# Hybrid decoder step, tail of the MoE: residual and expert rows of five token tiles summed by TensorE in PSUM

## The reference

```
h = x + concat(conv_out, rwkv_out) @ w_out
h = h + hier_moe(rmsnorm(h, norm2_g), ...)        # top-2 experts of a token
y = h * rsqrt(mean(h * h) + 1e-6) * norm_f_g      # final RMSNorm, per token
```

## Time and profile before

| | |
|---|---|
| time, median of 3 runs | 1180.86 us (1178.79 to 1181.15) |
| profiled execution: time | 1179.14 us |
| profiled execution: span of the core | 1177.4 us |
| busy: PE, DVE, ACT, POOL | 95%, 57%, 31%, 19% of the span |
| chain that ended last: PE, DVE, DMA | 81%, 9%, 4% of the span |
| granted TensorE clock, mean | 0.978 |
| y_rows reads (line 739) | 8 of 1024 KB and 1 of 512 KB |
| output writes (line 735) | 8 of 512 KB and 1 of 256 KB |

### The profile page before, as it was taken

How to read it: one execution, slowest core, us unless ns; L and a number is a source line. 1 busy time by engine, 2 the same in 40 slices (tenths; PEclk the granted TensorE clock), 3 DMA queues, 4 the chain that set the end, 5 groups by cost and what they waited for, 6 DMA issues and landing times.

```text
span 1177.4 us, 24390 instructions
## 1 busy us (share of the span) xinstructions
PE 1114.6 (95%) x9472; PEld 678.4 (58%) x9473; DVE 676.6 (57%) x1147; ACT 367.5 (31%) x722; POOL 223.6 (19%) x280
## 2 busy tenths in 40 slices
PE   6999999999998789999999999977999999999986
PEld 4666666666666789889894455544333333333362
DVE  6288999983554677888743232465343434334327
ACT  6000011011313657777551221022223232323233
POOL 7000000010002123322320001002233333323100
PEclk9999999999999899999999999977999999999999
DMA  9211111010000111111232421157998899999657
GB/s 290 72 36 36 36 36 45 18 42 23 1 1 6 18 20 20 18 17 18 48 111 98 130 72 36 45 208 295 388 349 322 310 333 340 415 417 400 258 187 311
DMA packets 97293, 171.44 MB, mean 146 GB/s; under 512 B 44377, under 2 KB 68624, under 8 KB 87921
## 3 DMA queue, kind: packets, MB, share of 16 engines
q1 hardware_dynamic: 89713, 152.31, 36.4%
q0 software_dynamic: 7488, 17.84, 4.3%
HBM read 153.63 MB, written 25.91 MB: 152 GB/s over the span
## 4 chain that ended last, share of the span: by engine, by line
PE 81%; DVE 9%; DMA 4%; issue 2%; ACT 2%; SPq 1%; DVEq 0%; ACTq 0%; POOLq 0%
PE ps L1630 27%; PE ps L2090 14%; PE ps L1940 9%; PE ps L2120 7%; PE ps L1642 6%; PE ps L1663 2%; PE ps L2077 2%; DMA arena<-in_w_exp_up_dram 2%; DVE arena L2419 1%; PE ps L2138 1%; PE ps L1970 1%; PE ps L1651 1%; DMA arena<-in_w_exp_down_dram 1%; DVE arena L2422 1%; PE ps L2147 1%
## 5 line engine op out<-in xcount | busy, mean ns | idle before, releaser
L1630 PE MATMUL ps<-arena 128*128 128x384 f32 (+1 forms) x1040 | 319.1, 468 | 0.0
L1630 PEld LDWEIGHTS ps<-arena 128*128 128x128 f32 x1040 | 196.9, 190 | 119.0 <-issue 1.9
L2090 PE MATMUL ps<-arena 128*64 x416 | 188.5, 596 | 3.1 <-DVE arena L2836 1.2
L2093 PE MATMUL ps<-arena 128*64 128x512 f32 x416 | 188.5, 596 | 0.0
L2233 DVE SCALAR_TENSOR_TENSOR arena<-arena,cw 128x1024 f32<-128x1024 f32 x240 | 168.2, 777 | 0.4
L2090 PEld LDWEIGHTS ps<-arena 128*64 128x64 f32 x416 | 54.4, 136 | 111.8 <-issue 111.7
L1940 PE MATMUL ps<-arena 128*128 128x512 f32 x256 | 113.1, 596 | 0.0
L1642 PE MATMUL ps<-arena 64*64 64x64 f32 x2960 | 100.8, 221 | 6.5 <-DMA arena<-x_blocks 2.1
L1642 PEld LDWEIGHTS ps<-arena 64*64 64x64 f32 x2960 | 94.0, 136 | 10.1 <-issue 5.1
L2120 PE MATMUL ps<-arena 128*64 x208 | 96.5, 607 | 2.4 <-ACT arena L1401 2.4
L2123 PE MATMUL ps<-arena 128*64 128x512 f32 x208 | 96.5, 607 | 0.0
(11 more groups left out here) (360 smaller groups left out, 1554.6 us busy)
## 6 DMA issues: line engine op xcount, KB each, us to landing
arena<-in_w_exp_gate_dram SPq DMA_DIRECT2D x32, 1024.0 KB, 8.2
arena<-in_w_exp_up_dram SPq DMA_DIRECT2D x32, 1024.0 KB, 11.3
arena<-in_w_exp_down_dram SPq DMA_DIRECT2D x32, 1024.0 KB, 10.2
arena<-in_w_in_dram SPq DMA_DIRECT2D x22, 512.0 KB, 4.1
arena<-in_x_prompt_dram SPq DMA_DIRECT2D x16, 512.0 KB, 7.9
arena<-y_rows SPq DMA_DIRECT2D x8, 1024.0 KB, 15.0
arena<-in_w_out_dram SPq DMA_DIRECT2D x2, 2048.0 KB, 10.7
xn_rows<-arena SPq DMA_DIRECT2D x8, 512.0 KB, 2.8
```

The source lines that it names most:

```text
L1630: ins = pe.matmul(banks(proj_bank(q) + piece)[:, 0:n1 - n0], win[q % 6][:, c, :], xnT[:, c, n0:n1], start=(c == 0), stop=(c == DC - 1))
L2090: pe.matmul(banks(b)[0:HS, :], xgT[b][:, c, 0:HS], wring_gu[:, bass.ds(slot, 1), 0:2, c, :].rearrange("p a w f -> p (a w) f"), start=(c == ...
L2093: ins = pe.matmul(banks(b)[HS:P, :], xgT[b][:, c, HS:P], wgu[b][:, :, c, :], start=(c == 0), stop=(c == DC - 1))
```

## The change

The residual of five tiles goes into PSUM as well, by an identity matmul, so that VectorE's addition for them is gone; ScalarE's square and VectorE's last multiplication then read these tiles from PSUM (`summed(i)`). TensorE's list has five tiles instead of six: tile 7 moves to VectorE. The identity multiplications ahead are 24 instead of 72, and the residual matmuls of the first four tiles follow them, before the waits for the diagonals and `yk`. The fifth tile (6) reuses the banks of tile 1, for which TensorE waits on `fin_done` 3. The order of processing becomes [0, 8, 1, 2, 3, 4, 5, 7, 6]; the reads keep their order, in a list READ of their own. On VectorE combine(0) and combine(8) come first, combine(4) after last_scale(2), and combine(7) after last_scale(5).

```diff
-        LAST = [0, NT - 1, 1, 2, 3, 4, *range(5, NT - 1)]
-        ON_PE = [1, 2, 3, 5, 6, 7]
+        READ = [0, NT - 1, *range(1, NT - 1)]
+        LAST = [0, NT - 1, 1, 2, 3, 4, 5, 7, 6]
+        ON_PE = [1, 2, 3, 5, 6]
+        ON_DVE = [i for i in LAST if i not in ON_PE]
...
+        def summed(i):
+            return banks(rows_bank(i), 2) if i in ON_PE else hres[i][0:rows_of(i), :]
...
@@ SP
-            for i in LAST:
+            for i in READ:
                 r = rows_of(i)
                 sp.dma_start(yk[i][0:r, :, :], y_pairs[i * P:i * P + r, :, :]).then_inc(yk_in[i], 16)
...
@@ ScalarE
-                act.wait_ge(ff_done, n + 1)
-                act.activation(fin_sq[i][0:r, :], hres[i][0:r, :], ACT.Square, accum_out=stat[0:r, 0, i:i + 1])\
+                if i in ON_PE:
+                    act.wait_ge(rows_psum, NT + ON_PE.index(i) + 1)
+                else:
+                    act.wait_ge(ff_done, ON_DVE.index(i) + 1)
+                act.activation(fin_sq[i][0:r, :], summed(i), ACT.Square, accum_out=stat[0:r, 0, i:i + 1])\
...
@@ TensorE
-            for n in range(72):
+            def residual_in(i):
+                for half in range(2):
+                    pe.matmul(banks(rows_bank(i) + half), ident[:, :], hres[i][:, half * 512:half * 512 + 512],
+                              start=True, stop=False)
+
+            for n in range(24):
                 pe.matmul(banks(7)[:, 0:P], ident[:, :], ident[:, :], start=True, stop=True)
+            for i in ON_PE[0:4]:
+                residual_in(i)
             for n, i in enumerate(ON_PE):
                 b = rows_bank(i)
                 pe.wait_ge(diag_ready, 2 + n)
+                if n == 4:
+                    pe.wait_ge(fin_done, LAST.index(ON_PE[0]) + 1)
+                    residual_in(i)
                 pe.wait_ge(yk_in[i], yk_0[i] + 16)
-                if n >= 4:
-                    pe.wait_ge(ff_done, LAST.index(ON_PE[n - 4]) + 1)
                 for half in range(2):
                     for k in range(TOPK):
                         ins = pe.matmul(banks(b + half), diag[:, k, i, :], yk[i][:, k, half * 512:half * 512 + 512],
-                                        start=(k == 0), stop=(k == TOPK - 1))
+                                        start=False, stop=(k == TOPK - 1))
                 ins.then_inc(rows_psum, 1)
...
@@ VectorE, combine(i)
-                if i in ON_PE:
-                    dve.wait_ge(rows_psum, NT + ON_PE.index(i) + 1)
-                    dve.tensor_tensor(hres[i], banks(rows_bank(i), 2), hres[i], ALU.add).then_inc(ff_done, 1)
-                    return
...
@@ VectorE, last_scale(n)
-                dve.wait_ge(ff_done, n + 1)
-                dve.scalar_tensor_tensor(out=fin[i][0:r, :], in0=hres[i][0:r, :], scalar=stat[0:r, 3, i:i + 1],
+                dve.scalar_tensor_tensor(out=fin[i][0:r, :], in0=summed(i), scalar=stat[0:r, 3, i:i + 1],
                                          in1=gain_f[0:r, :], op0=ALU.mult, op1=ALU.mult).then_inc(fin_done, 1)
 
-            for n in range(NT + 2):
-                if n < NT:
-                    combine(LAST[n])
-                if n >= 2:
-                    last_scale(n - 2)
+            combine(LAST[0])
+            combine(LAST[1])
+            for n in range(NT):
+                last_scale(n)
+                if n == 2:
+                    combine(4)
+                if n == 5:
+                    combine(7)
```

More of the change, by code:

```diff
@@ L493, in hybrid_decoder_step @@
         diag = at(O_ZS + NT * D, TOPK, NT, P)
-        LAST = [0, NT - 1, 1, 2, 3, 4, *range(5, NT - 1)]
-        ON_PE = [1, 2, 3, 5, 6, 7]
+        READ = [0, NT - 1, *range(1, NT - 1)]
+        LAST = [0, NT - 1, 1, 2, 3, 4, 5, 7, 6]
+        ON_PE = [1, 2, 3, 5, 6]
+        ON_DVE = [i for i in LAST if i not in ON_PE]
+        assert len(ON_PE) == 5 and len(LAST) == NT
         diag_ready, rows_psum = tanh_done, gb_psum
```

## The result

| | before | after |
|---|---|---|
| time, median (4 runs each) | 1180.11 us (1178.79 to 1181.15) | 1170.04 us (1167.56 to 1171.63) |
| ratio, 95% interval | | 0.9926 [0.9906, 0.9945] |
| profiled execution: time, span | 1179.14, 1177.4 us | 1171.15, 1169.4 us |

The kernel became faster in this comparison: the ratio is 0.9926, and the medians lie 10.1 us apart. Two later comparisons with the same changed program gave 0.9958 [0.9939, 0.9978] (after_again) and 0.9943 [0.9927, 0.9959] (after_again2). So the effect is nearer to 0.4 to 0.7%.

The account below looks back on a forecast made before the run. TensorE's late start and VectorE's load set the end, with reads beneath. Last read 1160.9 plus 10.6 us of writes gives 1171.5, span 1171.9 against 1177.4: 5.5 us less, 1175.4 from median 1180.86; range 1173.3 to 1178.0.

Parts of the forecast that it names:

- the residuals lie under the wait for tile 1: TensorE after the identities: four tiles' residuals, 6.9 us, cost nothing because tile 1's read lands only at 1144.9.
- A spell at half clock behind the pause: TensorE after its 1.8 us pause: one spell at 1.2 GHz takes 1.7 us of progress, hidden by the writes.
- PSUM operands cost the same: ScalarE's squares and VectorE's scalings reading PSUM: -0.04 to 0 and -0.06 to 0 us each, taken as 0.
- VectorE's load: VectorE in the tail: six additions gone, 6.8 us; tile 7 summed by itself added, 2.55 us.
- The writes last 10.6 us from the last read, and come last: Output writes queued behind the reads: from 1160.9 they take 10.6 us, the last landing at 1171.5, after the engines' 1171.1.
- The reads are unchanged, the last at 1160.9: Reads of the tail's tiles: same landings as before the change, 2.4 us apart, the last at 1160.9.
- The spread of 1180.86 (-2.1, +0.3): Whole kernel: the median before the change and its own spread, used for the forecast time and the range.
- reads did not give way to writes: Rival, DMA in the tail: earlier writes push tile 7's read to 1164.0, gain only 3.6 us, 1177.3; chance 0.12.
- PSUM reads did not slow each other: Rival, engines sharing PSUM: each of five scalings takes 1.2 us more, gain 2.2 to 2.5 us, 1178.4; chance 0.08.
- the clock did not stay at half: Rival, TensorE after its pauses: stays at 1.2 GHz, each tile 6.9 us, 11.2 us slower, 1192.1; chance 0.06.

Follow-up runs that it names:

- after72: The changed kernel with 72 identity matmuls again instead of 24; median 1179.40 us, ratio to the kernel before 1.0009, tail 48.99 us.
- after_dup: The changed kernel with one more 512 KB write, issued behind the first output write; median 1173.32 us, ratio to the kernel before 0.9962, tail 42.09 us.
- after_resdve: The changed kernel with VectorE adding the residual again, in the old VectorE call order; median 1177.76 us, ratio to the kernel before 0.9997, tail 47.81 us.
- after_act8: The changed kernel with tile 8's read issued by ScalarE on its own queue; median 1170.47 us, ratio to the kernel before 0.9938, tail 42.46 us.
- after0: The changed kernel without the 24 identity matmuls; median 1174.15 us, ratio to the kernel before 0.9951, tail 42.46 us.
- before24: The kernel before with 24 instead of 72 identity matmuls, nothing else changed; median 1178.60 us, ratio to before 0.9998, tail 47.90 us.
- before_wide: The kernel before with 19 identity matmuls of 512 columns replacing 72 of 128; median 1178.50 us, ratio to before 1.0005, tail 47.61 us.
- after_read8: The changed kernel with tile 8's read third instead of second; median 1173.04 us, ratio to the kernel before 0.9948, tail 41.07 us.

## Why the prediction was wrong

The direction and, in the tail, the resource that ends last were right; the time was 5.4 us too high. Two terms of the sum failed: the reads, which were taken as unchanged (1.1 us), and the spread of the total (-2.1, +0.3), under which the other 4.3 us fall. With the reads alone put right the range would still have missed the measured time. In the prediction's own steps:

- *TensorE: the residuals lie under the wait for tile 1.* Right. In the tail's time tile 1 starts at 15.1 (forecast 14.9), tiles 1, 2 and 3 are summed at 18.8, 22.2 and 25.7 (18.3, 22.2, 25.7 without the spell); after72 shows the price without the cover. Tile 5 came at 29.1, not 29.5, since its read was no longer late.
- *A spell at half clock behind the pause.* Wrong for this execution, whose granted clock stayed at 1.00. Of the profiles with a pause of 1.7 to 2.65 us (after, after_again, after_again2, after_dup, after_resdve, after_act8) one had a spell, of 1.5 us; those with 6.94 and 8.71 had one of 2.4. I said that the writes' queue hides it; with the reads sooner it hides only 0.6 us, and after_act8 and after0 ended 1.6 us later than after.
- *PSUM operands cost the same.* Right: 1284 and 1285 ns, so a PSUM operand costs the scaling nothing that shows; ScalarE's square takes 1024 against 1052.
- *VectorE's load.* The last scaling came at 37.2 us (37.9 forecast without the spell). But the account of what is gone (six additions, 6.8 us, for 2.55 of tile 7) leaves out a part that only the order of the scalings holds: those of tiles 0 and 8, 2.8 us, now run under VectorE's wait. after_resdve loses the whole gain with both; how much each is worth is open.
- *The cut from 72 to 24 identities alone* was not priced in the prediction as a part by itself; before24 shows that it gives no gain.
- *The writes last 10.6 us from the last read, and come last.* Right to 0.1 us; after_dup confirms that they come last.
- *The reads are unchanged, the last at 1160.9.* This is the step of the mechanism that failed. Relative to the first issue it came 1.1 us sooner, about 24.9 instead of 26.0. The 3.9 us between tiles 1 and 2 in the earlier trace rows, where every other spacing is 2.4, was the mark of it, and I took it for part of the reads. What stood there is one packet of instructions of 1.06 us, which was gone with the 48 identities (before24, after) and also with as much work in fewer instructions (before_wide). Since the writes end 10.6 us behind the last read, 5.5 + 1.1 = 6.6 us is the tail's gain, and the trace has 6.6.
- *The spread of 1180.86 (-2.1, +0.3).* This is the larger part of the miss. 1.4 us in the profiles and another 2.1 between the medians of four runs are not in the tail, and the median of before itself came out 0.75 lower (1180.11) than the 1180.86 that I started from: 1.1 + 1.4 + 2.1 + 0.75 = 5.4. The start of the tail moved by up to 12 us among kernels that are the same up to there, and the two later comparisons gave 6.3 and 7.7 us between medians. This suggests chance in the first comparison; most timed runs have no traces, so the cause of these 4.3 us stays open. My range took the spread from three runs of before, 2.4 us wide; 28 runs of it later lay between 1173.7 and 1183.2.

The rivals: reads did not give way to writes (the first write waited 14.3 us, and the reads of tiles 4, 5 and 6 landed 2.7 and 2.4 us apart), PSUM reads did not slow each other, and the clock did not stay at half.

A rival of another kind is untested: the kernel before with nothing changed but the order of calls on VectorE, so that tiles 0 and 8 are scaled ahead of the first addition. By the rows this could take up to 2.8 us off its end.

## What to carry to other kernels

Look at the landings of a row of equal transfers: a spacing that stands out is something else on one DMA engine, and may go with the edit. Filler matmuls held the clock here but need instructions, and a packet of instructions shares the DMA engines with the data. Useful work under a wait for data (here the residual) replaces part of the filler, and wide matmuls need fewer instructions; the residual alone was not enough (after0 paused for 6.94 us and lost 2.4 to the clock). Look also at what stands behind a wait in an engine's order of calls and could run under it. Where a change is worth less than the part ahead of it varies, compare the stretch that it touches in several profiles, and take the spread of the total from more than three runs.

## What the runs showed of the hardware

- A packet of the instruction queue (0.02 MB) took 1.06 us of one DMA engine in before. Tile 6's read landed 23.6 us behind the first issue with it and 22.5 in before_wide without it, with TensorE equally busy.
- While a read of 512 KB into 64 partitions was under way the engines moved 221 to 332 GB/s for 4 us with their share near 1 (after_read8; 266 and 270 in after), against 420 to 430 for reads into 128, wherever it stood in the order, and 254 to 303 on a queue of its own (after_act8). Over the 4 us of after_read8 this loses an estimated 1.4 us against 426 GB/s, about as much again as the 1.2 us that 512 KB take at that rate. The page SBUF — State Buffer of the Trainium skill, section Door 1: The DMA port swizzle, says that the first 64 partitions reach only half of the 16 ports; the dip agrees with that.
- Pauses of TensorE of 1.7 to 2.65 us mostly left the granted clock at 1.00 (five profiles of six); one of 2.55 us was followed by 1.2 GHz and cost 1.5 us (after_act8), and those of 6.94 and 8.71 us cost 2.4 each (after0, before24). Those of 1.85 and 2.41 us in the trace of before were followed by 1.2 GHz.
